# Strassen's scheme for the last three input slabs in a two-layer hybrid decoder step

## What is computed

```python
z = x @ P['w_in']                       # 544 x 1024 times 1024 x 3592
mq, mk, mv, mo, mi, mf, rq, rk, rv, rg, gx, gg, wz = jnp.split(z, splits, axis=-1)
hm, C1, n1, m1 = _mlstm(...)            # group A
y_m = jax.nn.sigmoid(mo) * (_head_norm(hm) * P['mlstm_g'])
ro, R1 = _retention(_rotary(rq, pos), _rotary(rk, pos), rv, R0)   # group B
y_r = jax.nn.silu(rg) * (_head_norm(ro) * P['ret_g'])
# group C: RG-LRU of gx, gated by gelu(gg);  group D: RWKV-7 (delta rule) of wz
mix = concat([y_m, y_r, y_g, y_w]) @ P['w_out']
```

## Time and profile before

| | us |
|---|---|
| median of three runs | 2244.63 (2242.76 to 2251.95) |
| profiled execution | 2241.11 |
| its span, first to last instruction | 2239.3 |
| mean granted clock of PE | 0.997 |

### The profile page before, as it was taken

How to read it: one execution, slowest core, us unless ns; L and a number is a source line. 1 busy time by engine, 2 the same in 40 slices (tenths; PEclk the granted TensorE clock), 3 DMA queues, 4 the chain that set the end, 5 groups by cost and what they waited for, 6 DMA issues and landing times. The chain is left out here.

```text
span 2239.3 us, 32769 instructions
## 1 busy us (share of the span) xinstructions
PE 2194.0 (98%) x13686; PEld 1627.9 (73%) x13686; DVE 1173.2 (52%) x2031; ACT 432.2 (19%) x919; POOL 115.6 (5%) x208
## 2 busy tenths in 40 slices
PE   7999999999999999999999999999999999999998
PEld 5877775547856888888988777655488478888888
DVE  5652236567466444675256422555765474448643
ACT  2332222021212222100023321221113022220000
POOL 0111101000000000000002112010001000000000
PEclk9999999999999999999999999999999999999999
DMA  7121014253442122222242112143345412223221
GB/s 275 64 76 40 24 42 116 94 179 141 184 165 94 52 99 76 76 76 76 76 134 76 39 41 59 39 124 115 116 150 213 159 62 75 76 78 106 80 76 40
DMA packets 136338, 217.31 MB, mean 97 GB/s; under 512 B 33672, under 2 KB 67776, under 8 KB 136064
## 3 DMA queue, kind: packets, MB, share of 16 engines
q1 hardware_dynamic: 133888, 211.02, 27.7%
q10 hardware_dynamic: 2304, 4.20, 0.5%
HBM read 198.39 MB, written 14.58 MB: 95 GB/s over the span
## 5 line engine op out<-in xcount | busy, mean ns | idle before, releaser
L736 PE MATMUL psum<-xT,ring 128*128 128x256 f32 (+1 forms) x768 | 222.1, 415 | 0.1
L2359 PE MATMUL psum<-tmp 128*128 128x272 f32 x768 | 181.2, 392 | 0.0
L2359 PEld LDWEIGHTS psum<-tmp 128*128 128x128 f32 x768 | 145.9, 190 | 30.1
L736 PEld LDWEIGHTS psum<-xT,ring 128*128 128x128 f32 x768 | 131.3, 189 | 35.2 <-issue 10.2
L686 PE MATMUL psum<-xT,ring 128*128 128x256 f32 (+1 forms) x512 | 120.4, 394 | 5.2 <-ACT big L1910 2.0
L733 PE MATMUL psum<-ring,ext 128*128 128x512 f32 x256 | 122.8, 616 | 0.0
L2451 PE MATMUL psum<-big,ring 128*128 128x256 f32 (+2 forms) x768 | 120.0, 318 | 0.0
L2451 PEld LDWEIGHTS psum<-big,ring 128*128 128x128 f32 x768 | 112.4, 191 | 6.8
L686 PEld LDWEIGHTS psum<-xT,ring 128*128 128x128 f32 x512 | 96.3, 190 | 26.6 <-issue 5.0
L2359 PE MATMUL psum<-xT,ring 128*128 128x272 f32 x448 | 107.4, 393 | 0.3 <-DMA ring<-in_w_up 0.3
L2359 PEld LDWEIGHTS psum<-xT,ring 128*128 128x128 f32 x448 | 85.0, 190 | 18.2 <-DMA ring<-in_w_up 0.8
(11 more groups left out here) (517 smaller groups left out, 3728.4 us busy)
## 6 DMA issues: line engine op xcount, KB each, us to landing
ring<-in_w_down SPq DMA_DIRECT2D x16, 2048.0 KB, 7.7
ring<-in_w_in SPq DMA_DIRECT2D x14, 2048.0 KB, 8.5
ring<-in_w_up SPq DMA_DIRECT2D x14, 2048.0 KB, 8.2
big<-in_cache_mem_k SPq DMA_DIRECT2D x16, 1024.0 KB, 7.5
ring<-in_xa_wk SPq DMA_DIRECT2D x4, 2048.0 KB, 8.4
ring<-in_xa_wv SPq DMA_DIRECT2D x4, 2048.0 KB, 10.3
ring<-in_w_out SPq DMA_DIRECT2D x4, 2048.0 KB, 9.7
ring<-in_xa_wq SPq DMA_DIRECT2D x4, 2048.0 KB, 11.0
```

Source lines behind the costliest of these rows:

```text
L736: ins = pe.matmul(bank[:, :c.stop - c.start], wring[:, n % 2, k, i * P:(i + 1) * P], xTv[:, k, c], start=(k == 0), stop=(k == KC - 1))
L2359: ins = pe.matmul(ps[:, :HT], left[:, k, :], right[:, k, :], start=(k == 0), stop=(k == KH - 1))
```

## The change

Slabs 4, 5, 6 become six pairs of feature tiles `u`, and each pair seven products of half size in both directions (4 contraction steps, 272 columns): 168 matmuls instead of 192. The sums of inputs are made once per layer (`zs_x_sum`, four of 128 x 1088) and the sums of weights per pair (`zs_w_sum`, four of 128 x 512), both on DVE, in buffers that are free at that time. The seven products of a pair go alternately to the two filler banks, and the later ones are added onto what the bank holds (no `start` for products 2, 4, 5, 6), while after each product a reader takes the bank's present sum: ACT copies it for products 0, 2, 3, 6, DVE adds it to the tile for 1, 4, 5. The gates become passes of ACT over two whole tiles (`zs_gate`).

```diff
+            def zs_w_sum(v, u, i):
+                w, s_ = wring[:, (4 + u // 2) % 2], zs_w[u % 2]
+                a, b = up_blocks(u)
+                if i == 0:
+                    slab_wait(v, 4 + u // 2)
+                if i in (1, 3):
+                    v.wait_ge(sig["zsw"], sig.at("zsw", 4 * u + i))
...
+            def zs_add(v, u, i):
+                t1, t2 = T_HALVES
+                dst = {1: z(4 + 2 * u)[:, t1], 4: z(5 + 2 * u)[:, t2], 5: z(4 + 2 * u)[:, t2]}[i]
+                ps = bk.take(v, ("zs", u, i))[:, :HT]
+                bk.given(v, ("zs", u, {1: 0, 4: 3, 5: 2}[i]))
+                bk.give(v.scalar_tensor_tensor(dst, ps, zs_scale(u), dst, ALU.mult, ALU.add), ("zs", u, i))
+            def zs_gate(s, u):
+                for i in (1, 4, 5, 6):
+                    bk.given(s, ("zs", u, i))
+                sig.up(s.activation(z(4 + 2 * u, 2), z(4 + 2 * u, 2), ACT.Sigmoid if u == 1 else ACT.Silu), "zgate")
...
-            SPARE = [(n, SLABS_IN[n][1] + i, half, k) for n in (4, 5, 6) for i in range(4) for half in range(2) for k in range(KC)]
+            SPARE = [("zs", u, i, k) for u in range(Z_PAIRS) for i in range(7) for k in range(KH)]
             Z_ITEMS = len(SPARE)
-            SPARE += [(n, None, nt, k) for n in range(7, 11) for nt in range(2) for k in range(KC)]
+            SPARE += [("kv", n, nt, k) for n in range(7, 11) for nt in range(2) for k in range(KC)]
...
+                        if k == 0:
+                            if i == 0 and u % 2 == 0:
+                                slab_pe(pe, 4 + u // 2)
+                            if i in (2, 3, 4, 5):
+                                pe.wait_ge(sig["zsw"], sig.at("zsw", 4 * u + {2: 2, 3: 1, 4: 3, 5: 4}[i]))
+                            if u == 0 and i in (2, 3, 4, 6):
+                                pe.wait_ge(sig["zsx"], sig.at("zsx", {2: 2, 3: 1, 4: 3, 6: 4}[i]))
+                            bk.begin(pe, key, (u + i) % 2)
+                        left, right = ((w[:, :KH, a], xTv[:, :KH, t1]), (w[:, KH:, a], xTv[:, KH:, t1]), (s_[1], zs_x[1]), (s_[0], zs_x[0]),
+                                       (s_[2], zs_x[2]), (s_[3], xTv[:, KH:, t2]), (w[:, KH:, b], zs_x[3]))[i]
+                        ins = pe.matmul(psum[:, (u + i) % 2, :HT], left[:, k, :], right[:, k, :], start=(k == 0 and i in (0, 1, 3)),
+                                        stop=(k == KH - 1), skip_group_check=True)
...
-                    spare_products(pe, "bonus", FILL_BONUS, (0, 2))
-                    finish_half(pe, "bonus", (0, 2))
+                    pe.wait_ge(sig["oc1"], sig.at("oc1", 2))
+                    ps = bk.begin(pe, ("orow1",), 5)
+                    bk.filled(pe.transpose(ps[:126, :P], oc1[:, :], ident), ("orow1",))
+                    spare_products(pe, "bonus", FILL_BONUS, (0, 1))
...
-                        spare_products(pe, ("dpad", T), 2, (0, 1))
+                        spare_products(pe, ("dpad", T), 3, (0, 1))
...
-                                spare_products(pe, ("dsc", T), 4, (0, 1))
+                                spare_products(pe, ("dsc", T), 5, (0, 1))
...
-                    spare_products(pe, ("D", 2), FILL_D[1], (0, 1))
+                    spare_products(pe, ("D", 2), FILL_D[1], (0, 3))
...
+                    zs_x_sum(v, 0)
+                    zs_x_sum(v, 1)
+                    zs_w_sum(v, 0, 0)
+                    zs_w_sum(v, 0, 1)
                     bk.given(v, ("wa", 1, 0))
...
                     sig.up(ins, "rk")
+                    v.wait_ge(sig["small_w"], sig.at("small_w", 16 * N_SMALL_W))
+                    drain(v, ("gates",), graw_rows)
+                    bk.take(v, ("orow1",))
+                    bk.give(v.tensor_copy(orow1[:126, :], psum[:126, 5, :P]), ("orow1",))
+                    zs_x_sum(v, 2)
+                    zs_w_sum(v, 0, 2)
...
                     sig.up(tt(z(ZK_D, 2), z(ZK_D, 2), X1, ALU.mult), "dfeat")
-                    v.wait_ge(sig["small_w"], sig.at("small_w", 16 * N_SMALL_W))
-                    drain(v, ("gates",), graw_rows)
+                    zs_add(v, 0, 1)
                     for i in range(2):
                         drain(v, ("bonus", i), lambda ps, c: tt(X5[:, i, c], ps, z(ZV_D + i)[:, c], ALU.mult))
...
+                    zs_w_sum(v, 0, 3)
+                    zs_x_sum(v, 3)
+                    spare_add, spare_sum = [2], [4]
+                    def spare_adds(point, sums):
+                        while spare_add[0] < min(HALF_DONE[point], Z_ITEMS // KH):
+                            _, u, i = GROUPS[spare_add[0]]
+                            if i in (1, 4, 5):
+                                zs_add(v, u, i)
+                            spare_add[0] += 1
+                        while sums and spare_sum[0] < 4 * Z_PAIRS:
+                            u, i = spare_sum[0] // 4, spare_sum[0] % 4
+                            if u > 1 and spare_add[0] <= 7 * (u - 2) + 5:
+                                break
+                            zs_w_sum(v, u, i)
+                            spare_sum[0] += 1
+                            sums -= 1
...
                             bk.give(tt(DmT[:n, :, :w], DmT[:n, :, :w], ps[:n, :, :w], ALU.subtract), ("DT", T, m))
+                            spare_adds(("X", T, m), 2)
...
                     out_slab(sp, 7)
-                    z_wait(sp, 11)
+                    z_wait(sp, 15)
```

More of the change, by code:

```diff
@@ new lines, in zs_scale, with zs_x_sum @@
+            def zs_scale(u):
+                return QSCALE if u == 3 else 1.0
+            def zs_x_sum(v, i):
+                t1, t2 = T_HALVES
+                x11, x12 = xTv[:, :KH, t1], xTv[:, :KH, t2]
+                x21, x22 = xTv[:, KH:, t1], xTv[:, KH:, t2]
+                if i in (1, 3):
+                    v.wait_ge(sig["zsx"], sig.at("zsx", i))
+                left, right = ((x12, x11), (x22, zs_x[0]), (x22, x12), (x21, zs_x[1]))[i]
+                sig.up(v.tensor_tensor(zs_x[i], left, right, ALU.subtract), "zsx")
@@ L724, in spare_products @@
                 while at < len(SPARE) and (units > 0 if upto is None else at < upto):
[L725 to L731, removed]
@@ L732, in spare_products @@
-                    if f is None:
+                    kind, n, half, k = SPARE[at]
+                    if kind == "kv":
+                        key = ("kv", n - 7, half)
+                        if k == 0:
+                            if half == 0:
+                                slab_pe(pe, n)
+                            bk.begin(pe, key, banks[half])
+                        bank = psum[:, bk.turn[key][0], :]
                         ins = pe.matmul(bank, memT[:, k, half * P:(half + 1) * P], wring[:, n % 2, k, :], start=(k == 0), stop=(k == KC - 1))
-                    else:
-                        c, i = HALVES[half][1], f - SLABS_IN[n][1]
-                        ins = pe.matmul(bank[:, :c.stop - c.start], wring[:, n % 2, k, i * P:(i + 1) * P], xTv[:, k, c],
-                                        start=(k == 0), stop=(k == KC - 1))
@@ L741, in spare_products @@
+                    units -= 2 if kind == "kv" else 1
                     at += 1
                 HALF_DONE["at"] = at
-                HALF_DONE[point] = at // KC
+                HALF_DONE[point] = groups_done(at)
             def finish_half(pe, point, banks, upto=0):
-                at = HALF_DONE["at"]
-                spare_products(pe, point, 0, banks, max(at + -at % KC, KC * upto))
+                at = HALF_DONE["at"] - Z_ITEMS
+                spare_products(pe, point, 0, banks, max(at + -at % KC, KC * upto) + Z_ITEMS)
@@ L1029, in _ @@
                     product(pe, ("gates",), 4, lambda k: graw, [const("gate_fold")])
[L1030 to L1031 removed]
+                    pe.wait_ge(sig["oc1"], sig.at("oc1", 2))
+                    ps = bk.begin(pe, ("orow1",), 5)
+                    bk.filled(pe.transpose(ps[:126, :P], oc1[:, :], ident), ("orow1",))
+                    spare_products(pe, "bonus", FILL_BONUS, (0, 1))
                     pe.wait_ge(sig["rk"], sig.at("rk", 1))
                     for i in range(2):
[L1034 to L1038 removed]
+                        for part, c in HALVES:
+                            ps = bk.begin(pe, ("bonus", i, part), 2 + i if part == 0 else 4 + 2 * i)
+                            bk.filled(pe.matmul(ps[:, :c.stop - c.start], const("sum64"), X5[:, i, c], start=True, stop=True), ("bonus", i, part))
                     for T in range(5):
@@ L1975, in _ @@
                         levels = (1, 2, 4, 8, 16, 32) if T < 4 else (1, 2)
+                        if T == 4:
+                            spare_tiles(("dpad", 4))
+                            zs_gate(s, 5)
                         spare_tiles(("dsc", T))
```

69 lines of the change are left out of this document (50 added, 19 removed).

## The result

The changed kernel takes **2308.54 us** (median of 6 runs, 2307.29 to 2309.42), the kernel before 2243.31 (6 runs, 2242.59 to 2251.95): ratio 1.0284, 95% interval 1.0268 to 1.0299, slower by 65 us. The forecast was 2297 in a range of 2260 to 2318. The profiled execution has a span of 2307.0 us against 2239.3, a difference of 67.7, and a mean granted clock of 0.979 against 0.997.

A forecast was written before the change was run, and what follows sets the result against it. PE's instruction stream was taken as the bound. Filler moves, tail gain, join, bank waits and slab wait gave +23.1 us per layer, +52.2 with the clock: span 2291.5, execution 2293.3, median forecast 2297 us, range 2260 to 2318.

The forecast's parts named there:

- What bounds the kernel: Whole span: PE's instruction stream, busy 98%; a change pays only if it shortens that stream without opening waits.
- Part 1, the move of the filler: Delta rule's token tiles: filler comes earlier in the list, +5.9 us per layer; it runs dry 19 kv items early.
- Part 1, the tail gain: End of the A/B stage: the last 19 kv fillers vanish, gaining 10.9 and 9.4 us in the two layers.
- Part 2, the join: Before the delta rule: PE's product 3 waits for DVE's reordered first add, +6.4 us per layer.
- Part 3, the banks: Delta rule: small waits for reads of the two filler banks used as accumulators, 6.7 us per layer.
- the banks serialise: Rival: piled products wait for their bank reads throughout, +25 us on the forecast, 2322 us; chance 0.03.
- Part 4, slab 9: kv filler at ("D", 2): PE waits for a load queued behind S-state stores, +15.0 and +13.5 us.
- The clock: One fall to PE's lower level at each of two long waits per layer, 6.0 us in all; bounds 0 and 9.
- The Trainium skill's rule: A DMA wait halves PE's rate at every return; extended to the A/B tail's DVE wait, +3 us, to 2300.
- slab 9 in time: Rival: the load lands before PE wants it, leaving only the join and small waits, 2265 us; chance 0.11.
- neither long wait: Rival: no long wait at join or slab, needing a DVE faster than its rows, 2250 us; chance 0.05.
- the faster one: Rival: DVE follows a faster PE in the A/B tail, so all 16.9 us of fill goes, 2223 us; chance 0.07.

The follow-up runs named there:

- e4_cut19: Kernel before the change, last nineteen 512-column filler matmuls of each layer cut to 16 columns, part of the result left out: 2239.64 us, ratio 0.9987.
- e8_groups: e3_warm plus two unused 512-column matmuls behind each of the four groups of 64x4 matmuls: 2310.25 us, ratio 1.0292.
- e2_join: Changed kernel with DVE's gates' copy, orow1 copy and two sums moved behind dfeat and the first add: 2291.71 us, ratio 1.0204.
- e1_slab9: Changed kernel with SyncE queuing slab 9 right behind slab 8, ahead of the S-state stores, in both layers: 2274.44 us, ratio 1.0129.
- e5_cut8: Kernel before the change, only the last eight 512-column filler matmuls of each layer cut to 16 columns, part of the result left out: 2251.26 us, ratio 1.0034.
- e3_warm: Changed kernel plus nine unused 512-column matmuls a layer where PE waits for DVE in the last two tiles: 2314.72 us, ratio 1.0295.
- e6_all: Changed kernel with e1_slab9, e2_join, slab sums between the masks, a later second gate and re-placed tail filler: 2238.23 us, again 2238.03 us.

## Why the prediction was right, and its step that was mis-sized

- **What bounds the kernel**: right. PE was the stream, and each new wait on it showed in full: 14.0 and 13.8 us at the slab, 6.4 us at the join.
- **Part 1, the move of the filler**: right. The list ran dry where the walk through it said: no kv filler behind the third chunk loop (its last group starts at 447.88 in layer 0). The delta rule took 11.5 us more in each layer, forecast 12.6 with the small waits.
- **Part 1, the tail gain** (10.9 and 9.4 us): **the step that was mis-sized**. Measured 3.5 and 1.7. Its first half, 1.5 us of DVE's slack, held: 15.04 us to the first group in the changed kernel, 15.0 in e4_cut19, against 16.7. Its second half took the eight fillers' busy time as gain, "and I see nothing that would be late there instead". Nothing was late; the rest ran at half its clock, for 6.6 us in layer 0 and 6.8 in layer 1 (e8_groups). In layer 0 that leaves 0.8 of the 7.4 missed. It lies in the first three chunk loops, and the trace has a wait of 0.78 us there, PE's for the kv copy at 422.54: a term that the prediction did count, in Part 3, and that the table above has in the row of the delta rule. The row was there to be read: the earlier trace rows has PEclk 0.89 in just this stretch of layer 0, with the fillers still in it. I priced that as one fall of 1.5 us at the two long waits, and none here.
- **Part 2, the join**: right in mechanism and size, 6.39 us for 6.4; e2_join took out 16.8 us for both layers. The clock cost 1.8 us there in layer 0, not 1.5. DVE's rows, put in their new order, gave the add's start as 163.8; it came at 166.05, later by the 2.25 us by which all of that execution was late.
- **Part 3, the banks**: right in kind and near in size, by the waits: the two of ("om", 0, 1) and ("om", 3, 1) 2.8 us together (2.6), UV 1.1 (1.5), ACT's gate 1.5 (1.7), the kv copy 0.8 (0.8). The rival that the banks serialise is out: the delta rule has only these waits beside the moved filler.
- **Part 4, slab 9**: right. 14.0 and 13.8 us for 15.0 and 13.5, and e1_slab9 took out 34.1 us, a little more than the waits and their clock (31).
- **The clock**: falls at the two long waits, as assumed, 16.5 us of slab stage for 15.5. Its bound of 9 us was too small: 13.4 us more were paid in the tails. (It is the same loss as that of the tail gain, not a second one.)
- The Trainium skill's rule that I had weighed (TensorE: Matmul & The Clock Gate, section "HAM oscillation — how this bites in real kernels") ties the return to half rate to a wait for a DMA. At slab 9 the trace agrees: 13.7 us at the lower level beside a wait of 14.0. The reach to the tail that the prediction gave it came out in kind, since the clock falls there in waits for DVE (at 460.6 and 1600.7), but not in size: 3 us were worked out, which gave 2300, and 13.4 were paid. In e5_cut8 the level fell with no wait over 1.1 us and stayed low for 34.1 us, which that rule doesn't cover, and the measurement decides.
- **The rivals**: slab 9 in time and neither long wait fell with the list of waits; the faster one with the first half of the tail. Its condition, that DVE follows a faster PE, was not met: in e4_cut19 DVE stayed busy 14.60 of 15.0 us, and 3.5 us came back in all.

The total came within 12 us because the tail's row alone was off by more than 2.6 us in a layer. The misses of the other rows nearly cancel over both layers: +3.6 at the join, 2.25 of it ahead of the part that the change touches, -2.2 in the delta rule, -0.6 at the slab. The range held the measured time since its upper end assumed half of the tail gain; its three terms add up to 2323 (12.6 + 3.0 + 10.2 above the forecast), not to the 2318 that stands there.

## What to carry to other kernels

When a change makes work finish earlier in a counted list, look at two things: which load in a fixed queue now has its first user ahead of its issue, and which stretch runs out of filler. Moving one load up, ahead of eleven stores, was worth 34 us; the scheme's whole saving was 22. Filler in a stretch of small matmuls is not free to take: price it by the granted clock that the stretch shows with it (0.89 here was the warning), and try the stretch without it (e5_cut8 is an edit of two lines) before the real change is built on the gain.

## What the runs showed of the hardware

- TensorE's granted clock was at its lower level for 34.1 us with no idle time over 1.1 us (e5_cut8), from 1.7 us into groups of 64x4 matmuls with only 16-column ones between. With two 512-column matmuls behind each group it stayed at 1.00 (e8_groups), even though PE did 7.9 us more work in the stretch. The kernel before, with two behind each group as well, has one fall of 3.4 us there in layer 0 and none in layer 1.
- Work taken away can cost time: with eight matmuls a layer cut from 512 to 16 columns the median was 2251 for 2243 us. Work added can be nearly free: eight more, in a stretch that took 15.7 us instead of 14.3 where their own time was 7.9.
- Near the edge the fall is not the same in each execution of one program: e5_cut8's times lie at 2240, 2250 and 2261 us, with mean granted clocks of 0.993, 0.989 and 0.983. What decides between them in one execution stays open.
- Why the lower level held for 34.1 us in e5_cut8 and 27.3 in e3_warm, into wide matmuls, but 23.9 in the changed kernel and 13.7 in layer 0 of e6_all, no run tells.
